# Where the sample value products stand on TensorE in the attention steps of a hybrid decoder layer

## The reference, cut to what matters

```python
def diff_attn_core(q, k, v, q_pos, k_pos, lam):
    ...
    p = jax.nn.softmax(s, axis=-1).reshape(b, DA_HEADS, 2, tq, tk)
    w = p[:, :, 0] - lam * p[:, :, 1]
    return jnp.einsum("bhqk,bkhd->bqhd", w.astype(v.dtype), v)
```

## Time and profile before

| | |
|---|---|
| median of 3 runs | 2849.26 us |
| profiled execution, its own time | 2848.53 us |
| span in the profile | 2846.7 us |
| TensorE busy | 2700.8 us (95%) |
| VectorE busy | 1378.2 us (48%) |
| ScalarE busy | 660.4 us (23%) |
| long steps 16 to 31 | about 1429 to 1567 us from the span's start |

### The profile page before, as it was taken

The page is one execution under the profiler, slowest core; times in us unless marked ns, Lnnn a source line. Parts: engine busy times, 40 slices in busy tenths (PEclk is TensorE's granted clock), DMA queues, the critical chain, the costliest instruction groups (busy, mean ns, idle before and its releaser), DMA issues.

```text
span 2846.7 us, 52037 instructions
## 1 busy us (share of the span) xinstructions
PE 2700.8 (95%) x21467; PEld 2560.6 (90%) x21467; DVE 1378.2 (48%) x1465; ACT 660.4 (23%) x1004; POOL 268.7 (9%) x258
## 2 busy tenths in 40 slices
PE   6999999999999999998777899869999999999998
PEld 6999999999999998997344899759999999999998
DVE  4332233223575588777666678675443323322333
ACT  5111111111311222332344232212222101211123
POOL 1000000000001123112000554200000000000000
PEclk8999999999999999998799999879999999999999
DMA  3111111111223445667865000133211111111112
GB/s 104 44 46 50 44 52 44 45 44 48 88 94 123 137 124 186 215 204 263 274 186 164 29 25 29 29 114 118 82 45 44 52 45 45 44 52 44 44 43 76
DMA packets 270206, 252.12 MB, mean 89 GB/s; under 512 B 20724, under 2 KB 216144, under 8 KB 269920
## 3 DMA queue, kind: packets, MB, share of 16 engines
q1 hardware_dynamic: 252960, 189.42, 22.3%
q0 software_dynamic: 16896, 60.40, 5.8%
q10 hardware_dynamic: 192, 0.07, 0.0%
HBM read 209.93 MB, written 39.90 MB: 88 GB/s over the span
## 4 chain that ended last, share of the span: by engine, by line
PE 87%; DVE 7%; ACT 1%; issue 1%; DMA 1%; SPq 1%; DVEq 0%; POOL 0%; ACTq 0%; POOLq 0%
PE ps L1783 74%; PE ps L2089 1%; PE ps L2104 1%; PE ps L2048 1%; PE ps L2109 1%; PE ps L1827 1%; PE ps L1990 1%; DMA value_ring<-in_cache_v 1%; PE ps L2013 1%; PE ps L1947 1%; PE ps L2144 1%; PE ps L2136 1%; SPq L559 0%; DVE small L1483 0%; SPq L560 0%
## 5 line engine op out<-in xcount | busy, mean ns | idle before, releaser
L1783 PE MATMUL ps<-h_hi,w_hi 128*128 128x344 f32 x3072 | 991.7, 323 | 10.3 <-DVE w_lo L1205 10.3
L1783 PE MATMUL ps<-h_lo,w_hi 128*128 128x344 f32 x3072 | 980.6, 319 | 0.0
L1783 PE MATMUL ps<-h_hi,w_lo 128*128 128x344 f32 x3072 | 980.3, 319 | 0.0
L1783 PEld LDWEIGHTS ps<-h_hi,w_hi 128*128 128x128 f32 x3072 | 577.8, 188 | 25.9 <-issue 19.8
L1783 PEld LDWEIGHTS ps<-h_lo,w_hi 128*128 128x128 f32 x3072 | 578.0, 188 | 2.1 <-issue 1.9
L1783 PEld LDWEIGHTS ps<-h_hi,w_lo 128*128 128x128 f32 x3072 | 577.9, 188 | 0.0
L1783 PE MATMUL ps<-ff_hi,w_hi 128*128 128x344 f32 x1056 | 337.1, 319 | 0.0
L1783 PE MATMUL ps<-ff_lo,w_hi 128*128 128x344 f32 x1056 | 336.6, 319 | 0.0
L1783 PE MATMUL ps<-ff_hi,w_lo 128*128 128x344 f32 x1056 | 336.2, 318 | 0.0
L838 ACT ACTIVATE w_hi<-w_stage 128x1024 fp32r<-128x1024 f32 x194 | 203.9, 1052 | 479.8 <-PE ps L1783 479.8
L1205 DVE TENSOR_TENSOR w_lo<-w_stage,w_hi 128x1024 fp32r<-128x1024 f32 x194 | 239.2, 1233 | 139.8 <-ACT w_hi L838 103.8
(11 more groups left out here) (409 smaller groups left out, 3243.7 us busy)
## 6 DMA issues: line engine op xcount, KB each, us to landing
w_stage<-in_ffn_up SPq DMA_DIRECT2D x176, 256.0 KB, 3.1
key_ring<-in_cache_k SPq DMA_DIRECT2D x128, 256.0 KB, 3.0
value_ring<-in_cache_v SPq DMA_DIRECT2D x128, 256.0 KB, 2.9
w_stage<-in_w_in SPq DMA_DIRECT2D x84, 256.0 KB, 3.3
w_stage<-in_ffn_down SPq DMA_DIRECT2D x80, 256.0 KB, 2.9
gate_save<-tmp POOLq DMA_DIRECT2D x16, 516.0 KB, 4.5
gate_ring<-gate_save POOLq DMA_DIRECT2D x16, 516.0 KB, 4.4
row_ring<-row_save SPq DMA_DIRECT2D x40, 128.0 KB, 2.9
```

The costliest lines, as they stand in the source:

```text
L1783: last = mm(dense[s][:, j], w[w0][:, k0 + k, :], r[:, k, j * CH:(j + 1) * CH], start=(k == 0 and n == 0), stop=(k == nk - 1 and n == 2))
```

## The change

In the long steps all fills but a sample's first one go from the late to the early place. A second fill (f % 4 = 1) goes with them only if it isn't in the same step as the first one. The short steps stay as they were.

```diff
@@ -2013,6 +2013,10 @@
                         last = mm(PSf[:, b:b + w], Q[q, h, qi * P:n], Kr[q, h, j:j + w],
                                   start=True, stop=True)
                 last.then_inc(ev["scores_done"], 1)
+            def early(f):
+
+                return f % 4 > 1 or (f % 4 == 1 and FILL_STEP[f - 1] < FILL_STEP[f])
+
             def square_sum(step, bank, at):
 
                 row = 32 * (step % HP)
@@ -2038,7 +2042,7 @@
                     elif t == qi:
                         last.then_inc(ev["w_trans_hi"], 1)
                 for k in range(4 * NS):
-                    if FILL_STEP[k] == step < FIRST and k % 4:
+                    if FILL_STEP[k] == step and early(k):
                         weight_values(k)
                 pe.wait_ge(*ev.at("w_moved", step + 1))
                 if step:
@@ -2052,7 +2056,7 @@
                     if FILL_STEP[4 * b + 3] == step - 1:
                         turn_sums(b)
                 for f in range(4 * NS):
-                    if FILL_STEP[f] == step and (step >= FIRST or f % 4 == 0):
+                    if FILL_STEP[f] == step and not early(f):
                         weight_values(f)
             pe.wait_ge(*ev.at("v_back", 16 * HP))
```

## The result

| | before | after |
|---|---|---|
| median | 2843.53 us (7 runs, 2839.59 to 2850.14) | 2855.79 us (7 runs, 2850.96 to 2860.66) |
| profiled execution, its own time | 2848.53 us | 2852.96 us |
| span in its profile | 2846.7 us | 2851.2 us |
| S(17) to the first product of the chunk loop | 138.8 us | 147.4 us |

The ratio is 1.0035, with a 95% interval of 1.0023 to 1.0047: the changed kernel is slower by some 10 us (7 to 13). The kernel before has four more runs than ahead of the prediction, and its median is lower for it: 2843.53 and not 2849.26 us. So the time that was named, 2858.6, lies 2.8 us above the measured median though the difference came out as forecast.

The account below looks back on a forecast made before the run. In attention iterations 17 to 29, VectorE's and ScalarE's own cycle and the value ring's round were taken to limit in turn. Order +6.8 and clock +2.6 gave +9.4 us: 2857.9, median 2858.6 us, range 2847 to 2870.

Parts of the forecast that it names:

- The early fill costs nothing when its pages are there: Between turns and column sum: ScalarE's copy leaves TensorE idle 0.85 to 1.17 us, which covers a fill.
- Five waits move ahead of V: In five long attention steps, column sum and V queue behind a fill waiting for pages; together 8.2 us lost.
- step 17: Attention iteration where fill 14 waits for its pages ahead of column sum and V; loss 1.5 us.
- step 20: Attention iteration where fill 18 waits for its pages ahead of column sum and V; loss 1.75 us.
- step 23: Attention iteration where fill 22 waits for its pages; loss between 0 and 1.75 us, taken as 0.9.
- step 26: Attention iteration where fill 27 waits for its pages while VectorE waits too; loss 2.0 us.
- step 28: Attention iteration where fill 30 waits for its pages ahead of column sum and V; loss 2.1 us.
- Step 24 gains 1.1 us, fill 17 0.3: VectorE's wait for S(26) shrinks and fill 17's slot, late in step 19, comes free sooner; together -1.4 us.
- the order part of the sum, 6.8: Long attention steps without the clock: 8.2 us lost less 1.4 us gained, +6.8 us.
- The clock: TensorE's clock around long pauses: between +10.0 us if each new one lowers it and -4.8; middle taken, +2.6.
- The case in which the clock falls at every pause: Rival for the long steps: 6.8 + 10.0 = +16.8 us, 2866 us; chance 0.2.
- Fills 14, 18, 27 and 30 land no sooner after their slot came free: Value ring in the long steps: these landing sooner after their slot came free would show the forecast wrong.

Follow-up runs that it names:

- only_ready: The kernel before with only fills 13, 15, 19, 23, 29 and 31, whose pages have landed, moved early in the long steps; ratio 1.0003 to the kernel before.
- the one-page pair: The kernel before and the changed one, each fill loading and using only its first page: ratios 0.9948 and 0.9947 to the kernel before.
- only_waiting: The kernel before with only page-waiting fills 14, 18, 22, 26, 27, 30, plus 13 and 29, moved early in the long steps; ratio 1.0033, +9.4 us.
- step_26: The kernel before with only fills 26 and 27 moved early in the long steps; one run with its profile, 2842.26 us.
- hoist_late: The kernel before, with SyncE reading a fill's four page numbers ahead of its wait for the slot; ratio 0.9982, -5 us.
- spread_late: The kernel before with its fills, all late in the long steps, spread over one step more; ratio 0.9967, -9 us.
- spread_hoist: spread_late with a fill's page numbers read ahead of SyncE's wait, as in hoist_late; ratio 0.996 to the kernel before, median 2832.61 us.
- hoist_early: The changed kernel, with SyncE reading a fill's four page numbers ahead of its wait; ratio 1.0009 to the kernel before, +2.6 us.

## Why the prediction was right

The predicted +9.4 us stands against a measured +10 (7 to 13), by the mechanism that was named. Point by point:

- *The early fill costs nothing when its pages are there.* Right: 1.84 us against 1.83 from turns to column sum, and only_ready and the one-page pair show no loss.
- *Five waits move ahead of V.* Right: only_waiting has the whole loss, only_ready none of it.
- *The size of each.* Taken at full clock, by taking off what fill, column sum, V and S took beyond their full-clock times in either trace: step 17 1.1 us (forecast 1.5), step 20 2.2 (1.75), step 23 2.6 (0.9), step 26 1.8 (2.0), step 28 2.1 (2.1). Their sum is 9.8 against 8.2. Part of these is only when the pages landed, counted from the S before: sooner than before by 0.4 us in step 17 and 0.1 in step 26, later by 0.5 in step 20, 0.9 in step 23 and 0.3 in step 28. With that set right they are 1.5, 1.7, 1.7, 1.9 and 1.7, in sum 8.5. In step 20 the 0.5 is what the wait of fill 17 had been: its removal came back there. In step 23 the 0.9 is the low clock of before, at which fill 21 and S(24) ran: it gave the load of fill 22 a head start, so that it landed 5.4 us after S(24) began, and 6.3 us after it in the changed trace. The one that was mis-sized is step 23, where I had taken half of a range from 0 to 1.75 and the upper end came true.
- *Step 24 gains 1.1 us, fill 17 0.3.* Neither is shown. In the trace 2.3 us are gone in step 24, of which about 1.6 are V(24) and its fill at the lower clock before. The rest goes without the early place as well: in step_26, where fill 23 stays late and S(25) comes late as here, S(25) to S(26) takes 6.80 us, against 6.78 in the changed kernel. This -1.4 is the term that the order part of the sum, 6.8, had wrong; the stage grew by 8.6 with about as much low clock in both traces.
- *The clock.* Its five falls cost about 8.0 us in the changed trace, by the same reckoning, 1.4 to 1.9 each: the forecast had 2.7 for a new one, but the clock was mostly back by the end of V. The falls of before, of about 7.8 us in sum (without step 31, which is slow in both), are gone or in other places, so in this pair of profiles the clock's term is near 0 and not +2.6. The case in which the clock falls at every pause came true in that, and its time of 2866 us did not, since the trace that it was added to held as much low clock of its own.
- *Whether the low clock of before was the order's.* This is open. The long stretch from 1477 stands also in the traces of hoist_late and spread_late, and not in those of step_26 and spread_hoist; it stands in none of after, only_ready, only_waiting and hoist_early. The profile of before is no typical one either: its mean clock over the whole kernel is 0.969, in a range of 0.968 to 0.976 (mean 0.972) over the 53 runs beside the experiments. The seven of the changed kernel have 0.966 to 0.973, mean 0.968. Among runs of one kernel (127 in all), 0.001 less goes with 0.9 us more; from that an estimate is that some 3 us of the measured 10 go with the clock. That is near the +2.6, but the +2.6 was the middle between +10.0 and -4.8, which nothing had singled out. That it came near is luck, and so is a part of how close +9.4 is to +10; the five places and their order price are not.
- *The waits of line 1990 above 17 us*: 21.6. *The stage 7 to 10 us longer*: 8.6. *Fills 14, 18, 27 and 30 land no sooner after their slot came free*: right but for 0.4 us at fill 14.

## What to carry to other kernels

Ahead of moving work into an idle slot of an in-order engine, look at what it waits for itself: the slot hides its busy time, and its wait is passed on to all that is queued behind. The price is the smaller of two times: the work that used to run during the wait, and the wait less the idle time that stood in the slot anyway. Beyond that it does not grow with the wait. If a ring limits, change when the slots are needed: spreading the uses over one step more gained 9 us (a part of it at the stage's end, for another reason) where moving them within the step lost 10.

## What the runs showed of the hardware

Four loads of 256 KB issued 1.1 us apart: the last of each four landed 2.6 to 3.7 us after its issue in the long steps of before, and up to 4.7 in only_ready. Issued 0.5 us apart, the last landed after 3.1 to 5.0 us (hoist_early). Closer issue bought 1.3 us of a round of 7.0 (fills 18, 22, 26 and 30), where 2.3 us of issue time were saved.

The granted clock fell at each of five pauses of 3.2 to 4.3 us, and also in places with no pause over 1 us (before, from 1477). Pauses of 2.1 to 2.8 us went either way. The stretch behind them was at 0.50 after 2.66 and 2.79 us in only_ready and after 2.13 in hoist_early, and at 1.00 after 2.16 in the kernel before, 2.36 in step_26, and 2.16 and 2.75 in hoist_early. The same untouched stretch ran at 0.71 in one profile and 0.83 in the other. A few us between two profiles may be nothing else.
